# Second block: one step of the recurrences per half piece of the projections; first norm: transposes ahead of the modulation's sums

## What is computed

```python
mod = silu(c) @ w_ada + b_ada                 # nine chunks of 1024: shift, scale, gate, three times
u = rmsnorm(h, norm_ff1) * (1 + sc1) + sh1
h = h + 0.5 * g1 * ((silu(u @ w_gate) * (u @ w_up)) @ w_down)
# second block, mixer
proj = rmsnorm(h, norm_mix_w) @ w_in          # q,k,v of GDN; gz; q,k of the mLSTM; its v; its output gate
g_qkv = silu(causal_conv4(g_qkv)); m_qk = silu(causal_conv4(m_qk))
a = strict_lower((beta*k) @ k.T * decay);  t_inv = inverse(a + 1)      # per head and chunk
go = rmsnorm(delta_rule(t_inv, q, k, v)) * silu(gz)
mh = rmsnorm(mlstm(mq, mk, mv, gates)) * sigmoid(mo)
h = h + concat(go, mh) @ w_out
```

## Time and profile before

| | us |
|---|---|
| median of three runs | 1756.5 (1756.46 to 1760.33) |
| the profiled execution | 1758.48 |
| its span, first to last instruction | 1757.1 |
| PE busy in it | 1502.3 (85%) |
| DVE, ACT, POOL busy | 1117.3, 735.5, 354.8 |
| mean granted TensorE clock | 0.948 |

### The profile page before, as it was taken

How to read it: one execution, slowest core, us unless ns; L and a number is a source line. 1 busy time by engine, 2 the same in 40 slices (tenths; PEclk the granted TensorE clock), 3 DMA queues, 4 the chain that set the end, 5 groups by cost and what they waited for, 6 DMA issues and landing times.

```text
span 1757.1 us, 21274 instructions
## 1 busy us (share of the span) xinstructions
PE 1502.3 (85%) x7804; PEld 1129.2 (64%) x7804; DVE 1117.3 (64%) x1911; ACT 735.5 (42%) x1576; POOL 354.8 (20%) x319
## 2 busy tenths in 40 slices
PE   6899998999889999688986884788878788878876
PEld 6789997889879999687976873433433343434322
DVE  6656666676665555576755546778585858677645
ACT  5444443535335444463332442453434444343433
POOL 0000001000010000101200002354444445453441
PEclk9899998999999999898998997999999999999999
DMA  8777775676456555332321524999999999999996
GB/s 312 298 273 239 253 239 192 219 224 200 175 194 175 180 182 191 132 120 76 99 85 43 177 86 148 392 423 421 420 421 421 420 421 421 413 421 421 420 422 270
DMA packets 91452, 467.32 MB, mean 266 GB/s; under 512 B 10738, under 2 KB 11155, under 8 KB 57939
## 3 DMA queue, kind: packets, MB, share of 16 engines
q0 software_dynamic: 39072, 279.19, 39.3%
q1 hardware_dynamic: 50960, 184.57, 31.3%
q10 hardware_dynamic: 1314, 2.18, 0.4%
HBM read 461.71 MB, written 4.19 MB: 265 GB/s over the span
## 4 chain that ended last, share of the span: by engine, by line
PE 56%; DVE 22%; DMA 11%; ACT 6%; issue 4%; POOL 1%; SPq 0%; ACTq 0%; DVEq 0%; POOLq 0%
DMA Ft<-peer_uv,ids 9%; DVE Ft L1757 8%; PE ps L408 8%; PE ps L409 8%; PE ps L410 8%; PE ps L1075 6%; PE ps L452 3%; PE ps L453 3%; PE ps L454 3%; PE ps L525 2%; PE ps L526 2%; PE ps L527 2%; PE ps L391 2%; PE ps L720 2%; PE ps L827 1%
## 5 line engine op out<-in xcount | busy, mean ns | idle before, releaser
L1075 PE MATMUL ps<-Ft 128*128 128x512 f32 x800 | 385.9, 623 | 116.0 <-ACT Ft L2248 115.3
L1099 DVE TENSOR_TENSOR wlo<-raw,whi 128x1024 fp32r<-128x1024 f32 x268 | 324.0, 1234 | 135.6 <-ACT whi L1783 135.0
L408 PE MATMUL ps<-uhi,whi 128*128 128x256 f32 x1280 | 372.1, 291 | 4.4 <-DVE wlo L1099 4.4
L1075 PEld LDWEIGHTS ps<-Ft 128*128 128x128 f32 x800 | 147.8, 195 | 339.9 <-ACT Ft L2248 202.7
L409 PE MATMUL ps<-ulo,whi 128*128 128x256 f32 x1280 | 364.3, 285 | 0.0
L410 PE MATMUL ps<-uhi,wlo 128*128 128x256 f32 x1280 | 364.0, 284 | 0.0
L1757 DVE CUSTOM_DVE_ANT_0 Ft<-Ft 128x1024 f32<-128x1024 f32 x200 | 245.2, 1226 | 102.7 <-DMA Ft<-peer_uv,ids 92.2
L2371 POOL DMA_INDIRECT Ft<-peer_uv,ids x200 | 231.5, 1157 | 300.6 <-PE ps L1075 266.1
L1783 ACT ACTIVATE whi<-raw 128x1024 fp32r<-128x1024 f32 x268 | 270.7, 1047 | 46.5 <-PE ps L454 27.2
L408 PEld LDWEIGHTS ps<-uhi,whi 128*128 128x128 f32 x1280 | 247.8, 194 | 10.5 <-issue 8.0
L409 PEld LDWEIGHTS ps<-ulo,whi 128*128 128x128 f32 x1280 | 247.6, 193 | 3.8 <-issue 2.2
(11 more groups left out here) (368 smaller groups left out, 2171.3 us busy)
## 6 DMA issues: line engine op xcount, KB each, us to landing
raw<-ff_gu SPq DMA_DIRECT2D x88, 512.0 KB, 4.8
raw<-w_ada SPq DMA_DIRECT2D x72, 512.0 KB, 5.0
raw<-ff_dn SPq DMA_DIRECT2D x44, 512.0 KB, 4.6
raw<-w_in SPq DMA_DIRECT2D x32, 512.0 KB, 3.6
raw<-w_in_s SPq DMA_DIRECT2D x28, 512.0 KB, 4.8
raw<-w_out SPq DMA_DIRECT2D x16, 512.0 KB, 3.6
raw<-peer_wq SPq DMA_DIRECT2D x16, 512.0 KB, 4.6
raw<-w_in_m SPq DMA_DIRECT2D x12, 512.0 KB, 4.5
```

Of the source, the lines that this page charges most:

```text
L408: t.matmul(o, hi[:, c], x[0][:, i], start=(k == 0), stop=False)
L1075: ins = t.matmul(acc[r * 2 + c], diag[n % NDIAG], gbuf[n % NGAT][:, 1024 + c * 512:1024 + (c + 1) * 512], start=first, stop=last)
L1099: v.tensor_tensor(lo, raw_slot(j), hi.bitcast(F32), ALU.subtract).then_inc(*up("lo", j))
```

## The change

Four edits.

1. In the second block `tick` runs twice per piece: a new argument `between` of `cols` and `rows` takes a step in the middle of each piece on PE (before step k = 4 of a column tile; after half r = 0 of a row part), and on DVE and ACT right after the piece's `take()`, ahead of its evacuation.
2. The GDN generators stop after the seventh round until "mx" is set, that is until the `mx` tiles are through (so that the transposes and what follows run beside `mlv`). The mLSTM joins before `mo` instead of after it.
3. In `memory_kv` `norm_start("ff1")` stands before `ada_poll` on PE and DVE. `ffn(0)` runs its first three tiles one after the other, with LOOK = 2.
4. The five DMAs of constants go from ACT's queue to POOL's, behind the two rows of `b_ada` and ahead of the wait for `vRc`.

With two ticks per piece, `gz` takes steps 1 to 8, `mx` 0 to 5 take `i` in their middle and the next `y` at their end, `mx` 6 the last `i`; `mlv` takes steps 22 to 25 in its first two parts; `mo` takes the mLSTM's steps 1 to 4, at the ends of its parts.

```diff
-        def col_tile(o, j, x, ready=None):
+        def col_tile(o, j, x, ready=None, between=None):
             t.wait_ge(*at("lo", j))
             for k in range(8):
+                if k == 4 and between:
+                    between()
                 ins = col_k(o, j, x, k, ready)
...
-        def rows(name, n, x, ready, emptied, after=None):
+        def rows(name, n, x, ready, emptied, after=None, between=None):
...
                         ins = row_part(spot[name, i, r], j, x, r, [2 * part, 2 * part + 1], 8,
                                        ready if not i and not r else None)
+                        if r == 0 and between:
+                            between()
...
         def ffn(which, name):
+            firsts = [(name, "g", 0), (name, "u", 0), (name, "g", 1)]
             if which == 0:
                 ready = [("ulo", name, k // 2) for k in range(8)]
+                for key in firsts:
+                    j, _ = cur.take()
+                    col_tile(bank(key)[:, 0:256], j, u, ready)
+                    ready = None
             else:
                 ada_poll()
-                ready = norm(name, h)
-            firsts = [(name, "g", 0), (name, "u", 0), (name, "g", 1)]
-            col_group(firsts, u, ready)
+                col_group(firsts, u, norm(name, h))
...
                 yield
+            while "mx" not in st:
+                yield
             o = bank("g_kT", 2)
...
                 if i:
+                    norm_start("ff1", h)
                     ada_poll()
-                    norm_start("ff1", h)
                     cur.ahead(3)
...
-            rows("gz", 1, u, None, "gza", tick)
-            cols("mx", 8, u, None, "pad", tick)
-            rows("mlv", 1, u, None, "mlvc", tick)
-            rows("mo", 1, u, None, "moa", tick)
+            rows("gz", 1, u, None, "gza", tick, tick)
+            cols("mx", 8, u, None, "pad", tick, 0, tick)
+            st.add("mx")
+            rows("mlv", 1, u, None, "mlvc", tick, tick)
+            gens.append(mlstm())
+            rows("mo", 1, u, None, "moa", tick, tick)
             st.add("mix")
-            gens.append(mlstm())
             while gens:
                 tick()
```

On DVE (ACT has the same in `cols`, `rows`, `ffn`, the generator and the calls):

```diff
-        def rows(n, evac=None, after=None):
+        def rows(n, evac=None, after=None, between=None):
             for i in range(n):
                 for part in range(4):
                     j = take()
+                    if between:
+                        between()
                     if after:
                         after()
...
-            js = [take(NSPL - 1 - i) for i in range(3)]
+            js = [take(NSPL - 1 - i if which else LOOK) for i in range(3)]
...
+            norm_start("ff1")
             ada_poll()
-            norm("ff1", gain3[:, 0, :], modc9[:, 0, :], ("mod", 1, "gain"))
+            lows(cur.ahead(3))
+            norm_rest("ff1", gain3[:, 0, :], modc9[:, 0, :], ("mod", 1, "gain"), u[1], u[0])
```

And the constants:

```diff
-            if which == 0:
-                for key, dst, src in (("cst", cst[:, 128:C_SIZE], D["consts"][:, 128:C_SIZE]),
...
-                    a.dma_start(dst, src).then_inc(*land(key))
-            else:
+            if which:
                 norm(name, *coefs)
...
         row("bg5", G[1], D["b_ada"][5:6, :], 1024)
+        for key, dst, src in (("sw0", sw[:, 0:128], D["w_in_glr"]), ("sw1", sw[:, 128:256], D["w_in2_16"]),
+                              ("cst", cst[:, 128:C_SIZE], D["consts"][:, 128:C_SIZE]),
+                              ("wlr", wlr[0:16, :], D["w_gla_lr"]), ("bgl", bgl[0:1, :], D["b_gla_lr"])):
+            p.dma_start(dst, src).then_inc(*land(key))
         p.wait_ge(*at("vRc", 1, 1))
```

More of the change, by code:

```diff
@@ L429, in col_group, with cols @@
                         ins.then_inc(*up("tile", j))
-        def cols(name, n, x, ready, emptied, after=None, group=0):
+        def cols(name, n, x, ready, emptied, after=None, group=0, between=None):
             keys = [(name, i) for i in range(n)]
@@ L439, in cols @@
                 j, _ = cur.take()
-                col_tile(bank(keys[i])[:, 0:256], j, x, ready if not i else None)
+                col_tile(bank(keys[i])[:, 0:256], j, x, ready if not i else None, between)
                 give(keys[i], emptied, name, i)
@@ L1186, in norm, with cols @@
             norm_rest(name, gcol, scol, coefs, x[1], x[0])
-        def cols(n, evac=None, after=None, group=0):
+        def cols(n, evac=None, after=None, group=0, between=None):
             js = [take(NSPL - 1 - i) for i in range(group)]
@@ L1607, in gate_o @@
                 v.tensor_tensor(mo[:, r, :], mo[:, r, :], mln, ALU.mult).then_inc(*up("moa_v", r))
-            rows(1, gate_z, tick)
-            cols(8, conv("mx", 12, 8), tick)
-            rows(1, None, tick)
-            rows(1, gate_o, tick)
+            rows(1, gate_z, tick, tick)
+            cols(8, conv("mx", 12, 8), tick, 0, tick)
+            st.add("mx")
+            rows(1, None, tick, tick)
+            gens.append(mlstm())
+            rows(1, gate_o, tick, tick)
             st.add("mix")
-            gens.append(mlstm())
             while gens:
@@ L1833, in norm, with cols, rows @@
             norm_rest(name, gcol, scol, coefs, x[0])
-        def cols(n, evac, after=None, group=0):
+        def cols(n, evac, after=None, group=0, between=None):
             js = [take(NSPL - 1 - i) for i in range(group)]
             for i in range(n):
-                evac(i, js[i] if i < group else take())
+                j = js[i] if i < group else take()
+                if between:
+                    between()
+                evac(i, j)
                 if after and i >= group:
                     after()
-        def rows(n, evac, after=None):
+        def rows(n, evac, after=None, between=None):
             for i in range(n):
@@ L1867, in ffn @@
             coefs = gain3[:, which, :], modc9[:, 3 * which, :], ("mod", 3 * which + 1, "gain")
-            if which == 0:
-                for key, dst, src in (("cst", cst[:, 128:C_SIZE], D["consts"][:, 128:C_SIZE]),
-                                      ("sw0", sw[:, 0:128], D["w_in_glr"]), ("sw1", sw[:, 128:256], D["w_in2_16"]),
-                                      ("wlr", wlr[0:16, :], D["w_gla_lr"]), ("bgl", bgl[0:1, :], D["b_gla_lr"])):
-                    a.dma_start(dst, src).then_inc(*land(key))
-            else:
+            if which:
                 norm(name, *coefs)
-            js = [take(NSPL - 1 - i) for i in range(3)]
+            js = [take(NSPL - 1 - i if which else LOOK) for i in range(3)]
             for f in range(22):
@@ L2138, in gate @@
                 return evac
-            rows(1, gate(gz, "gz", ACT.Silu), tick)
+            rows(1, gate(gz, "gz", ACT.Silu), tick, tick)
             evac, done = conv("mx", mx, 8)
-            cols(8, evac, tick)
+            cols(8, evac, tick, 0, tick)
             done()
-            rows(1, lambda i, r, j: copy(mlv[:, r, :], spot["mlv", i, r], j, "mlvc", "mlv", i, r), tick)
-            rows(1, gate(mo, "mo", ACT.Sigmoid), tick)
+            st.add("mx")
+            rows(1, lambda i, r, j: copy(mlv[:, r, :], spot["mlv", i, r], j, "mlvc", "mlv", i, r), tick, tick)
+            gens.append(mlstm())
+            rows(1, gate(mo, "mo", ACT.Sigmoid), tick, tick)
             st.add("mix")
-            gens.append(mlstm())
             while gens:
```

## The result

| | kernel before | changed kernel |
|---|---|---|
| median, us | 1757.99 (20 runs) | 1764.43 (20 runs) |
| ratio | | 1.0034, 95% interval 1.0025 to 1.0042 |
| profiled execution, time | 1758.5 | 1763.4 |
| its span / mean granted clock | 1757.1 / 0.948 | 1762.1 / 0.942 |

The ratio leaves out one of the twenty times of the kernel before, 2743.0 us. The forecast was 1752.0; the time is 0.4 us above the range's upper end and has the other sign. Measured again beside the experiments, on the chips numbered 8 and 7, the same kernel gave 1.0012 (0.9999 to 1.0025) and 1.0036 (1.0023 to 1.0049, five executions; its medians differ by 4.0 us). So two of three measurements show it slower, by 4 to 6 us, and the third can't tell it from no change: how much it is differs by more than a single session's interval says.

What follows compares the result with a forecast made beforehand. PE bounds the kernel (busy 1502.3 of 1757.1 us), so only its idle time can be won: 1758.5 - 3.0 (first norm and tiles) - 1.5 (second mixer) = 1754.0, less 2.0 from profiled execution to median: 1752.0; 8-in-10 range 1745 to 1764.

Steps and rivals of the forecast that it cites:

- the other sign: Whole kernel: the prediction claimed a faster time, 1752.0 against a median of 1756.5; chances faster 0.38, slower 0.16, same 0.46.

Runs made afterwards that it cites:

- one was worth -4.6 us: Kernel before plus only first norm's transposes ahead of the sums, first three tiles singly, constants' DMAs on POOL; 0.9974 and 0.9975 of the kernel before.
- hidden by the other: Kernel before plus only a step per half piece in the second mixer and the mLSTM joining behind mlv; 1.0025 of the kernel before, median 1763.6.

## What to carry to other kernels

Finer interleaving left the sum of the waits nearly as it was (31.0 and 30.2 us) and moved them; its price was the clock of the products behind them, 7.4 us for the same 978. When steps are rearranged, price the products of one column and the broadcasts that come to stand together at both of their lengths, and keep both ends in the range. Ahead of them 0.9 us of spare products in a wait went with 7.4 us instead of 12.1 in three profiles of three, but the time they win, some 3 us, is at the edge of what was measured; in the tail, 7.5 us of them won nothing. And measure the parts of a change alone: here one was worth -4.6 us and hidden by the other. Compare stretches of unchanged code too: they differ between executions by as much as the change.

## What the runs showed of the hardware

- The clock is worth 5 to 6 us in identical code: 1398 products in 209.1 or 215.0 us; 64 last products in 7.3 or 12.1.
- Unchanged code of some 4350 products, from the first down product to `gz`, took 682.2, 685.0 to 685.6, 686.5 to 686.6 or 690.9 to 691.0 us in eighteen profiles, and nothing between.
- A program's time on one core can fall in groups, though it need not: the changed kernel's twelve times on one chip were six of 1756.9 to 1758.6 and six of 1761.6 to 1768.3, while its twenty of the result show no such gap; the profiles of an execution of 1755.8 and of two above 1763 are told apart by the clock at the last products and by where `gz` starts.
- Filling a 4.4 us wait kept the clock for the products behind it (2.05 instead of 3.78 us); filling a wait ahead of one-column products with 3.5 us of dense ones didn't (5.96 against 5.94).
- A VectorE operation with both inputs in SBUF took 2.37 us instead of 1.22 when it met GpSimd's masking (814.48 to 816.85 us); the one with an input in PSUM just ahead of it, met by the same masking, did not get longer (1.22).
